# RWKV first pass: scores ahead of its turned rows and bonus, blocks picked from the scores' tile, and the solved blocks' DRAM layout turned round

## The reference

```python
kk = kk / max(norm(kk), 1e-12)
k  = k * (1 + (a - 1) * k_a)
def step(S, (r, w, k, v, kk, a)):          # per head, S is 64 x 64
    sa = S @ -kk
    S  = S * w + outer(sa, kk * a) + outer(v, k)
    return S, S @ r
y = groupnorm(y) + (r * k * r_k).sum(-1) * v   # the last term is the "bonus"
```

## Time and profile before

| what | value |
|---|---|
| median of 3 runs | 1648.95 us (1648.46 to 1651.88) |
| the profiled execution's own time | 1648.68 us |
| its span | 1646.9 us |
| PE busy | 1604.4 us (97%), 9162 products |
| DVE busy | 1254.2 us (76%) |
| ACT busy | 990.4 us (60%) |
| POOL busy | 104.5 us (6%) |
| load of `solved`, issue to landing, median | 5.9 us, 4 times |
| stores to `blocks_out`, issue to landing, medians | 3.4 us (`own`), 2.4 us (`step`), 4 times each |

### The profile page before, as it was taken

How to read it: one execution, slowest core, us unless ns; L and a number is a source line. 1 busy time by engine, 2 the same in 40 slices (tenths; PEclk the granted TensorE clock), 3 DMA queues, 4 the chain that set the end, 5 groups by cost and what they waited for, 6 DMA issues and landing times.

```text
span 1646.9 us, 24651 instructions
## 1 busy us (share of the span) xinstructions
PE 1604.4 (97%) x9162; PEld 1349.8 (82%) x9162; DVE 1254.2 (76%) x1168; ACT 990.4 (60%) x936; POOL 104.5 (6%) x208
## 2 busy tenths in 40 slices
PE   8989999999999999999999999999999999999996
PEld 8878778778887997877788888888888888888885
DVE  5766774765446768486568898888989899898986
ACT  5553464454444654463447777677767777777774
POOL 0040240000000030150000000000000000000000
PEclk9999999999999999999999999999999999999998
DMA  9444443565554644443469999999999999898993
GB/s 297 134 140 155 125 140 123 198 202 181 185 195 149 203 140 134 130 149 128 167 226 328 335 393 355 359 367 332 394 331 367 354 358 392 322 373 327 392 365 117
DMA packets 218927, 414.29 MB, mean 252 GB/s; under 512 B 11104, under 2 KB 85472, under 8 KB 218336
## 3 DMA queue, kind: packets, MB, share of 16 engines
q1 hardware_dynamic: 214096, 400.97, 68.8%
q10 hardware_dynamic: 2256, 8.82, 1.4%
q0 software_dynamic: 2496, 3.43, 0.9%
HBM read 408.18 MB, written 2.62 MB: 249 GB/s over the span
## 4 chain that ended last, share of the span: by engine, by line
PE 81%; DVE 8%; issue 3%; ACT 2%; DMA 2%; POOL 2%; SPq 0%; DVEq 0%; ACTq 0%; POOLq 0%
PE W L535 17%; PE W L537 17%; PE W L536 17%; PE Y L535 7%; PE Y L537 7%; PE Y L536 7%; PE Y L823 1%; PE W L733 1%; DVE w_lo L1852 1%; DVE sc L2000 1%; DMA raw<-w_in 1%; POOL own L1791 1%; POOL step L1787 1%; ACT w_hi L1299 1%; DMA solved<-blocks_out 1%
## 5 line engine op out<-in xcount | busy, mean ns | idle before, releaser
L535 PE MATMUL W<-w_lo,x_hi 128*128 128x512 f32 x1104 | 441.8, 400 | 1.5 <-DVE x_lo L2187 0.9
L537 PE MATMUL W<-w_hi,x_hi 128*128 128x512 f32 x1104 | 432.4, 392 | 0.0
L536 PE MATMUL W<-w_hi,x_lo 128*128 128x512 f32 x1104 | 431.8, 391 | 0.0
L1852 DVE TENSOR_TENSOR w_lo<-raw,w_hi 128x2048 fp32r<-128x2048 f32 x112 | 256.8, 2295 | 188.8 <-ACT w_hi L1299 187.5
L1859 DVE TENSOR_TENSOR w_lo<-raw,w_hi 128x2048 fp32r<-128x2048 f32 x144 | 329.8, 2290 | 46.4 <-ACT w_hi L1305 46.4
L1305 ACT ACTIVATE w_hi<-raw 128x2048 fp32r<-128x2048 f32 x144 | 276.0, 1917 | 71.8 <-PE Y L537 40.0
L1859 DVE TENSOR_TENSOR w_lo<-raw_more,w_hi 128x2048 fp32r<-128x2048 f32 x120 | 275.0, 2292 | 25.7 <-ACT w_hi L1305 25.0
L1305 ACT ACTIVATE w_hi<-raw_more 128x2048 fp32r<-128x2048 f32 x120 | 230.4, 1920 | 64.8 <-PE W L537 42.1
L1299 ACT ACTIVATE w_hi<-raw 128x2048 fp32r<-128x2048 f32 x112 | 214.2, 1913 | 78.4 <-PE W L537 43.3
L535 PEld LDWEIGHTS W<-w_lo,x_hi 128*128 128x128 f32 x1104 | 208.2, 189 | 46.6 <-issue 4.5
L537 PEld LDWEIGHTS W<-w_hi,x_hi 128*128 128x128 f32 x1104 | 208.0, 188 | 44.9
(11 more groups left out here) (350 smaller groups left out, 1815.9 us busy)
## 6 DMA issues: line engine op xcount, KB each, us to landing
raw<-w_in SPq DMA_DIRECT2D x123, 512.0 KB, 4.6
raw<-moe_down SPq DMA_DIRECT2D x48, 1024.0 KB, 5.7
raw<-moe_gate SPq DMA_DIRECT2D x40, 1024.0 KB, 6.7
raw_more<-moe_gate SPq DMA_DIRECT2D x40, 1024.0 KB, 7.2
raw<-moe_up SPq DMA_DIRECT2D x40, 1024.0 KB, 7.4
raw_more<-moe_up SPq DMA_DIRECT2D x40, 1024.0 KB, 7.2
raw_more<-moe_down SPq DMA_DIRECT2D x40, 1024.0 KB, 6.6
raw<-w_branch SPq DMA_DIRECT2D x24, 512.0 KB, 4.3
```

Of the source, the lines that this page charges most:

```text
L535: nc.tensor.matmul(out_ap, lhs[0], rhs[1], start=start, stop=False)
L536: nc.tensor.matmul(out_ap, lhs[1], rhs[0], start=False, stop=False)
L537: return nc.tensor.matmul(out_ap, lhs[0], rhs[0], start=False, stop=stop)
L1852: V.tensor_tensor(w_lo[u % 3][:], raw[u % 3][:], w_hi[u % 3][:].bitcast(F32), ALU.subtract)\
```

## The change

In the list, the first pass's `scores` come directly behind unit conv 0, `pick` behind the second `scores`, and `compact`, `tok` and `bonus` behind the back of conv 1. The waits move with them: for p = 0, `tok` waits for the last `sc` of its pass (it uses the same PSUM banks), and `scores` no longer waits for tok and bonus but for `prep`; the first `mx` takes over these waits. The low part two units ahead is made in conv 1's back. `pick` reads `sc` in two halves of 64 partitions and writes to `dsh`. The four additions to `own_blocks` move to the first `knorm`. `blocks_out` is laid out so that the load has one 1 KB piece per partition, and each store 64 B pieces. List and `LATE_LOW` hold for both layers, the layout and `pick` for all four passes.

```diff
@@ -153,9 +153,9 @@
     ("units", "rkv", 3, 4), ("ss", 0), ("knorm", 0), ("shift", 2),
     ("units", "rkv", 4, 5), ("spread", 0), ("kk", 0), ("spill",),
     ("units", "rkv", 5, 6), ("prep", 0), ("decayed", 0),
-    ("units", "conv", 0, 1), ("tok", 0), ("bonus", 0),
-    ("front", "conv", 1), ("scores", 0, 0), ("back", "conv", 1), ("scores", 0, 1), ("compact", 0),
-    ("pick", 0), ("front", "conv", 2), ("back", "conv", 2), ("shift", 3),
+    ("units", "conv", 0, 1), ("scores", 0, 0),
+    ("front", "conv", 1), ("scores", 0, 1), ("pick", 0), ("back", "conv", 1), ("compact", 0), ("tok", 0), ("bonus", 0),
+    ("front", "conv", 2), ("back", "conv", 2), ("shift", 3),
     ("front", "conv", 3), ("back", "conv", 3), ("lora_w", 1), ("rate_w", 1), ("shift", 4),
     ("front", "conv", 4), ("back", "conv", 4), ("lora_a", 1), ("rate_a", 1), ("ksq", 1), ("decay", 1),
     ("front", "conv", 5), ("exps", 1), ("back", "conv", 5), ("ss", 1), ("knorm", 1), ("shift", 5),
@@ -187,7 +187,7 @@
 )
 
 
-LATE_LOW = (("qkv", 4), ("gate2", 3))
+LATE_LOW = (("conv", 1), ("qkv", 4), ("gate2", 3))
 SHIFT_ORDER = {e[1]: i for i, e in enumerate(e for e in TIMELINE if e[0] == "shift")}
 
 
@@ -281,7 +281,7 @@
         Y = [nc.alloc_psum_tensor(f"Y{i}", [P, 512], F32) for i in range(4)]
         E = nc.alloc_psum_tensor("E", [P, 512], F32)
         spill = nc.dram_tensor("x_spill", (T, D), F32, kind="Internal").ap()
-        blocks_out = nc.dram_tensor("blocks_out", (2, 8, P, BS), F32, kind="Internal").ap()
+        blocks_out = nc.dram_tensor("blocks_out", (P, 2, 8, BS), F32, kind="Internal").ap()
 
         ident = cst[:, C_ID:C_ID + P]
         blk = cst[:, C_BLK:C_BLK + P]
@@ -786,6 +786,8 @@
                 n = 2 * l + p
                 pe.wait_ge(sem("prep_ready"), n + 1)
                 pe.wait_ge(sem("kk_ready"), n + 1)
+                if p == 0:
+                    pe.wait_ge(sem("score_ready"), 8 * n + 8)
                 if n:
                     pe.wait_ge(sem("yrow_ready"), n)
                 nc.tensor.matmul(Y[3][:], blk, td[:].rearrange("p m t -> p (m t)"), start=True, stop=True)\
@@ -801,8 +803,10 @@
             def scores(l, p, c):
                 n = 2 * l + p
                 pe.wait_ge(sem("decayed_ready"), n + 1)
-                pe.wait_ge(sem("tok_ready"), n + 1)
-                pe.wait_ge(sem("bonus_ready"), n + 1)
+                if p:
+                    pe.wait_ge(sem("tok_ready"), n + 1)
+                    pe.wait_ge(sem("bonus_ready"), n + 1)
+                pe.wait_ge(sem("prep_ready"), n + 1)
                 if n:
                     pe.wait_ge(sem("pass_done"), n)
                 for m in range(2):
@@ -1793,12 +1799,12 @@
                     pool.wait_ge(sem("blocks_made"), made + 2 * m)
                 nc.gpsimd.memset(own[:].rearrange("p j t -> p (j t)")[:, ::BS + 1], 1.0).then_inc(sem("blocks_made"), 1)
                 pool.wait_ge(sem("blocks_made"), SOLVED * (n + 1) - 1)
-                pool.dma_start(by_block(blocks_out[0]), own[:].rearrange("p j t -> p (j t)")).then_inc(sem("blocks_moved"), 16)
+                pool.dma_start(blocks_out[:, 0].rearrange("(b j) u t -> u b j t", j=BS), own[:]).then_inc(sem("blocks_moved"), 16)
                 nc.gpsimd.tensor_copy(step[:], own[:].rearrange("p j t -> p t j")).then_inc(sem("blocks_made"), 1)
                 pool.wait_ge(sem("blocks_made"), SOLVED * (n + 1))
-                pool.dma_start(by_block(blocks_out[1]), step[:].rearrange("p j t -> p (j t)")).then_inc(sem("blocks_moved"), 16)
+                pool.dma_start(blocks_out[:, 1].rearrange("(b j) u t -> u b j t", j=BS), step[:]).then_inc(sem("blocks_moved"), 16)
                 pool.wait_ge(sem("blocks_moved"), 16 * (LEGS * n + LEGS - 1))
-                pool.dma_start(solved[:], blocks_out.rearrange("s u j t -> j s u t")).then_inc(sem("blocks_moved"), 16)
+                pool.dma_start(solved[:], blocks_out).then_inc(sem("blocks_moved"), 16)
 
             def swap(l, s):
 
@@ -1947,6 +1953,10 @@
             def knorm(l, p):
 
                 n = 2 * l + p
+                if n == 0:
+                    dve.wait_ge(sem("cst_full"), 96)
+                    for v, other in ((1, 0), (1, 2), (1, 3), (1, TOP)):
+                        link(V.tensor_tensor(own_blocks, cm[:, v, :], cm[:, other, :], ALU.add))
                 dve.wait_ge(sem("norm_ready"), n + 1)
                 link(V.tensor_scalar(inv[:], inv[:], 1e-12, None, ALU.max))
                 V.reciprocal(inv[:], inv[:]).then_inc(sem("inv_norm_ready"), 1)
@@ -1991,9 +2001,6 @@
 
             def scores(l, p, c):
                 n = 2 * l + p
-                if n == 0 and c == 0:
-                    for v, other in ((1, 0), (1, 2), (1, 3), (1, TOP)):
-                        link(V.tensor_tensor(own_blocks, cm[:, v, :], cm[:, other, :], ALU.add))
                 si = cst[:, C_SI:C_SI + 2 * P].unsqueeze(1).to_broadcast([P, 2, 2 * P])
                 for u in range(4 * c, 4 * c + 4):
                     dve.wait_ge(sem("score_done"), 8 * n + u + 1)
@@ -2003,9 +2010,11 @@
             def pick(l, p):
 
                 n = 2 * l + p
-                dve.wait_ge(sem("ac_ready"), n + 1)
-                picked = t3[:].rearrange("p m (u t) -> p (m u) t", t=HD)
-                link(V.tensor_tensor(picked, ac[:], own_blocks.unsqueeze(1).to_broadcast([P, 8, HD]), ALU.mult))
+                picked = dsh[:].rearrange("p m (u t) -> p (m u) t", t=HD)
+                for half in HALVES:
+                    last = V.tensor_tensor(picked[half], sc[half, :, 0, half], own_blocks[half].unsqueeze(1).to_broadcast([HD, 8, HD]),
+                                           ALU.mult)
+                link(last)
                 V.reduce_sum(diag[:], picked.rearrange("p u (b t) -> p u t b", b=NB), AX.X).then_inc(sem("blocks_made"), 1)
 
             def place(l, p):
```

## The result

The changed kernel takes 1654.49 us (median of 20, 1651.24 to 1657.69), the kernel before, run beside it, 1650.10 (20 runs, 1648.31 to 1654.15): ratio 1.0025, 95% interval 1.0019 to 1.0032. Forecast was 1642.8 and faster. The profiled execution has a span of 1649.4 us, against 1646.9 before; it took 1651.24, the shortest of the 20, so its rows show less than what the median lost.

A forecast was written before the change was run, and what follows sets the result against it. PE was taken to bound the kernel, losing time in waits for the inverse at the first mx and at the lower clock behind them. 4.6 + 2.6 + 1.0 + 0.15 - 1.0 - 1.2 = 6.15 us won: 1642.8, range 1640.6 to 1646.8.

The forecast's parts named there:

- Starting the solve earlier: First passes, scores to diag: earlier scores and pick bring diag 5.4 us earlier in layer 0, 5.6 in layer 1.
- From diag to the inverse: POOL's solve up to the stores: shifted, it meets more DVE splits and takes 1.5 us longer (0 to 4).
- The way back: Stores and load of the inverse through DRAM: 4.5 + 0.3 + 2.2 = 7.0 us, 1.6 won in layer 0, nothing in layer 1.
- What that does at place: First passes, mx to cg: waits for the inverse end, 4.6 and 2.6 us won; PE newly waits about 1 at cg.
- (D): Rival: DVE does not hold PE at cg, so PE wins its full 5.6 and 3.4 us: 1641; chance 0.10.
- (a) to (e): Side effects: 1.0 us lost at knorm, 1.2 in second passes; sc waits win 1.0 and 0.15; tok, bonus, LATE_LOW cost nothing.
- (a): First knorm: the four cm additions in front of its maximum lose 1.0 us, once.
- (e): Second passes: pick in two operations instead of one, before PE's pr waits, loses 0.6 us per layer, 1.2 in all.
- (A): Rival: inverse still late in layer 0, from solve or stores, DVE waits 1 to 3 us more: 1644 to 1646; chance 0.15.
- (B): Rival: PE's clock falls behind longer waits at knorm's spread or pr, up to 1.7 us each: 1644.5 or 1646.2; chance 0.16.
- (C): Rival: 64 B stores land late; slower from x = 9.1 us after the second's issue, 1654.8 at 10.6; chance 0.07.

The follow-up runs named there:

- e6: Changed kernel with DVE's splits in units conv 2 to 5 done on 64 columns only, so work is left out; 1643.06 us, ratio 0.9947.
- e5: Changed kernel with stores and load all in 1 KB pieces, blocks not rearranged and so in wrong places; 1641.18 us, ratio 0.9940.
- e13: Changed kernel with SP's weight loads held back until the first pass's inverse has landed; 1647.95 us, ratio 0.9979.
- e7: Changed kernel with the first seven of the fourteen rounds of POOL's solve left out, inverse wrong; 1640.11 us, ratio 0.9932.
- e3: Changed kernel with the four own_blocks additions behind decay and the second passes' pick in one operation again; 1652.01 us, ratio 1.0008.
- e9: e8 with DVE's splits of units conv 2 to 5 in four instructions of 512 columns; 1637.95 us, 0.9921 of the kernel before.
- e1: Changed kernel with the old layout of blocks_out, order, picks and additions as changed; 1647.90 us, 0.9983 of the kernel before.
- e8: e4 with the inverse's load in two halves, each waiting for its own store; 1642.43 us, 0.9945 of the kernel before.
- e4: e3 with the old layout of blocks_out; 1646.01 us, 0.9968 of the kernel before.

## Why the prediction was wrong, step by step

- **Starting the solve earlier: right.** 73.1 for `diag` against 73.7, both picks 0.70 and the sum 1.04 long. In layer 1 POOL starts 4.0 us earlier while everything before it is 1.3 later: 5.3 against 5.6.
- **From diag to the inverse: right in kind, half the size.** One split more is met, as the step says, and it costs 2.9 us (layer 1: 16.6 against 14.1, 2.5), not 1.5; inside its bounds of 0 to 4. In layer 1 the first round also begins 9.5 us after the first DMA of `diag`, 1.4 more than before.
- **The way back: the step that failed.** "After, the load has 128 pieces of 1 KB, as the stores had: 2.2 us" is its length with little else on the DMA engines (2.3 and 2.4 in e6 and e5, share 0.2). In the changed kernel it is issued 0.8 to 1 us behind a weight load of SP and takes 4.9 and 4.8; with that load held back (e13) 2.4. The sum had looked at the pieces of the transfer and not at SP's queue beside it. The stores took 5.2 and 5.0 us, not 4.5, and each was issued in 1.16 instead of 0.59 us, so the second starts 0.6 later; this price was left out. The legs came to 5.20 + 0.28 + 4.89 = 10.4 us where 7.0 was forecast and 8.6 was before. The load is the largest term, 2.7 and 2.6 us, but not the whole miss: e13, without it, takes 1647.95, which is 6.5 of the 11.7 us between forecast and median, and DVE still waits 2.0 and 1.9 us there.
- **Together in layer 0**: 112.41 at the landing against 107.7: solve +1.4, issue +0.6, store +0.7, load +2.7, `diag` -0.6. The spare time was to be 1.4, with DVE ready at 109.12 as before. But DVE's queue had moved up too, to 107.93, so 0.2 was left; the sum had kept the old time. Layer 1: 4.0 won at the start, then lost 1.4 + 2.5 on the way to the stores, 0.7 in a pause of POOL before the first store, 0.6 in its issue and 2.9 at the second store: 4.1 behind at the load's issue.
- **What that does at place: right in kind, not reached.** e7 shows it: 4.6 (with some luck, above) and 2.3 us won, against 4.6 and 2.6, and PE's new wait at cg is 0.4 us, not 1.0. PE's full 5.6 of rival (D) was not to be had.
- **(a) to (e): right.** The wait at `spread` is 1.7 us (1.8 forecast), the `sc` waits are gone, no wait at `tok`, `bonus` or conv 1's split; 3.1 and 3.2 us at `pr` against 3.0. Taking (a) and (e) back is worth 2.5 to 2.8 us against 2.2; e3's expectation had 2.2 to 3.4 more for falls of the clock that would end, and they did not all end.
- **The rivals.** (A) is what happened in layer 0 and, unforeseen, in layer 1. (B) happened at the two waits for `pr` (205 and 724). It is not bound to the longer waits: the clock falls at the `pr` waits also in e9, at 199 and 711, where they are 1.3 us at the longest, and in e1's layer 1, where one is 1.83, it does not. (C) had the right sign and half of the mechanism. It was to turn at x = 9.1 us of the store alone, and the change is slower at x = 5.2, since solve, issue and the load behind SP add to it. By the rule of the Trainium skill, "DMA: Bandwidth & Descriptors", section "Specifications", transfers under 512 B are read and written again. The row of 104 to 106, share 0.75 at 24 GB/s, fits with that, though no row shows a second read; e5's second store, in 1 KB pieces, lands in 3.2 us.

From the late landing to the end: layer 0's mx starts 0.7 us earlier than before, the `pr` waits and the fall of the clock behind them bring the second pass 1.1 us late, and layer 1's mx is 4.4 late, its router 5.7. Before's execution gives 2.7 us of this back at its very end: it pauses 4.5 us before the last products, the changed kernel's 1.8. So the spans differ by 2.5 and the medians by 4.4.

## What to carry to other kernels

- Laying data out so that the other transfer has the small pieces moves the cost; ask which of the two stands on the critical path and how each is issued. If both do, start the second as soon as half of the first is there (e8), on a semaphore for each.
- A transfer's length is not that of its bytes and pieces alone. Before shifting one, look at what the other queues issue at its new time: 0.8 to 1 us behind a weight load, the load of the inverse took twice as long (4.9 against 2.4 us). A load that is not needed soon can be held back for it (e13: 6.5 us).
- When the work before a wait moves up, the engine that waits may move up with it: take its new time for the spare time, not the old one.
- When two engines shut each other out by the instruction, cutting the long one in four is cheap where its engine has idle time (2.50 us for 2.29), and lets the short ones through (e9 against e8: 4.5 us).

## What was not expected of the hardware

- Exclusion by the instruction looks mutual: in e9, beside a row of four DVE pieces POOL's 0.3 us operations take 0.63, and DVE's row grows from about 2.5 us to 2.9 and 3.28. The Trainium skill, "SBUF — State Buffer", section "Who interferes with whom", has a two-input DVE instruction contend with a POOL one that reads SBUF, and calls the ports that they share an exclusive lock. Rows of both kernels agree: the changed kernel's three POOL operations of 2.25 to 2.43 us each end within 0.2 us of a split.
- A POOL store with 1024 pieces of 64 B takes 1.16 us to issue, one with 64 pieces of 1 KB 0.59; a load with 1024 pieces of 64 B takes 0.9 (e9). With the new layout POOL also pauses 1.0 us before the first store in two of its four passes:

```profile
POOL blocks_out L1802 <- issue: 2.3, 2, 1.3
```

  No kernel with the old layout shows it, and DVE is idle at that time in layer 1 (617.0 to 619.8). Its cause was not tried.
- At the `pr` waits PE's clock falls in some executions and not in others with the same waits (1.3 us at the longest): not in before's and e8's profiled execution, at both in e9's, in one layer each in e3's and e4's. The median of a kernel has some of each.
